# Folding the conditioning sums from 128 lanes to 64 before they are transposed

## The reference

```
def adaln(cond, w_ada, b_ada):
    return jnp.split(jax.nn.silu(cond) @ w_ada + b_ada, ADA_CHUNKS, axis=-1)

m_lat = [m[:, None, :] for m in adaln(c, w_ada[l], b_ada[l])]
m_ctx = adaln(c_ctx, w_ada[l], b_ada[l])
```

## Time and profile before

| | us |
|---|---|
| median of 3 runs | 2838.33 (2838.24 to 2838.36) |
| the profiled execution | 2838.6 |
| its span from first to last instruction | 2837.0 |
| PE busy in it | 2818.5 |
| DVE busy | 2005.0 |
| ACT busy | 1365.0 |

### The profile page before, as it was taken

One profiled execution on the slowest core, in us unless ns is written; L12 is line 12 of the kernel. 1 busy time (PEld: TensorE's weight loads), 2 busy tenths in 40 slices (PEclk: granted clock), 3 DMA queues, 4 the chain that ended last, 5 costly groups with the idle time before them and its releaser, 6 DMA issues.

```text
span 2837.0 us, 33955 instructions
## 1 busy us (share of the span) xinstructions
PE 2818.5 (99%) x13151; PEld 2333.5 (82%) x13151; DVE 2005.0 (71%) x2614; ACT 1365.0 (48%) x1733; POOL 23.5 (1%) x47
## 2 busy tenths in 40 slices
PE   9999999999999999999999999999999999999999
PEld 7888888888888888788888788888878888888887
DVE  6876799999877668756647888877765655655444
ACT  6655544444443447632334666654454444444333
POOL 2000000000000000000000000000000000000000
PEclk9999999999999999999999999999999999999999
DMA  7545687887878778456646544457767777776564
GB/s 258 151 134 178 186 258 251 255 257 248 259 248 271 268 256 264 147 160 189 178 145 187 151 120 126 119 188 260 232 191 228 223 223 226 225 228 201 191 192 153
DMA packets 299952, 583.18 MB, mean 206 GB/s; under 512 B 18394, under 2 KB 18802, under 8 KB 299153
## 3 DMA queue, kind: packets, MB, share of 16 engines
q1 hardware_dynamic: 296896, 572.01, 64.6%
q0 software_dynamic: 2320, 7.96, 0.9%
q10 hardware_dynamic: 576, 1.05, 0.1%
HBM read 578.85 MB, written 2.10 MB: 205 GB/s over the span
## 4 chain that ended last, share of the span: by engine, by line
PE 94%; DVE 3%; ACT 1%; issue 1%; DMA 1%; SPq 0%; ACTq 0%; DVEq 0%
PE psum L566 22%; PE psum L563 22%; PE psum L565 22%; PE psum L636 3%; PE psum L638 3%; PE psum L637 3%; PE psum L3099 2%; PE psum L3101 2%; PE psum L3100 2%; PE psum L511 1%; PE psum L513 1%; PE psum L512 1%; PE psum L3119 1%; PE psum L591 1%; PE psum L3159 1%
## 5 line engine op out<-in xcount | busy, mean ns | idle before, releaser
L719 DVE TENSOR_TENSOR w_lo<-w_raw,w_hi 128x1024 fp32r<-128x1024 f32 x776 | 945.7, 1223 | 607.8 <-ACT w_hi L713 603.9
L713 ACT ACTIVATE w_hi<-w_raw 128x1024 fp32r<-128x1024 f32 x776 | 821.9, 1060 | 1085.1 <-PE psum L566 1015.7
L563 PE MATMUL psum<-w_hi,x_split 128*128 128x512 f32 x1880 | 737.3, 392 | 0.0
L566 PE MATMUL psum<-w_hi,x_split 128*128 128x512 f32 x1880 | 732.3, 390 | 0.0
L565 PE MATMUL psum<-w_lo,x_split 128*128 128x512 f32 x1880 | 731.8, 389 | 0.0
L566 PEld LDWEIGHTS psum<-w_hi,x_split 128*128 128x128 f32 x1880 | 352.9, 188 | 73.7
L563 PEld LDWEIGHTS psum<-w_hi,x_split 128*128 128x128 f32 x1880 | 353.1, 188 | 71.6 <-DVE x_split L2597 0.3
L565 PEld LDWEIGHTS psum<-w_lo,x_split 128*128 128x128 f32 x1880 | 353.2, 188 | 71.5
L563 PE MATMUL psum<-w_hi,hidden_split 128*128 128x512 f32 x704 | 274.9, 390 | 0.0
L566 PE MATMUL psum<-w_hi,hidden_split 128*128 128x512 f32 x704 | 274.0, 389 | 0.0
L565 PE MATMUL psum<-w_lo,hidden_split 128*128 128x512 f32 x704 | 273.9, 389 | 0.0
(11 more groups left out here) (405 smaller groups left out, 3619.1 us busy)
## 6 DMA issues: line engine op xcount, KB each, us to landing
w_raw<-in_w_in SPq DMA_DIRECT2D x216, 512.0 KB, 3.6
w_raw<-in_w_ada SPq DMA_DIRECT2D x192, 512.0 KB, 4.8
w_raw<-in_w_ffn_up SPq DMA_DIRECT2D x176, 512.0 KB, 4.5
w_raw<-in_w_ffn_down SPq DMA_DIRECT2D x88, 512.0 KB, 5.5
w_raw<-in_w_ff_gate SPq DMA_DIRECT2D x88, 512.0 KB, 4.2
w_raw<-in_w_ff_up SPq DMA_DIRECT2D x88, 512.0 KB, 4.2
w_raw<-in_w_ff_down SPq DMA_DIRECT2D x88, 512.0 KB, 4.7
w_raw<-in_w_out SPq DMA_DIRECT2D x64, 512.0 KB, 4.7
```

The costliest lines, as they stand in the source:

```text
L563: nc.tensor.matmul(to, x_hi[:, tokens], hi, start=u == 0 and t == 0, stop=False, skip_group_check=True)
L566: mm = nc.tensor.matmul(to, x_lo[:, tokens], hi, start=False, stop=end and t == 1, skip_group_check=True)
L713: nc.scalar.activation(w_hi[:, b.slot(n)], raw[:, b.raw_slot(k)], ACT.Copy).then_inc(w_rounded, 1)
L719: nc.vector.tensor_tensor(w_lo[:, slot], raw[:, b.raw_slot(k)], r(w_hi[:, slot]), ALU.subtract).then_inc(w_split, 1)
```

## The change

Before a sum is transposed, its 128 partitions are folded to 64. The 512 columns are seen as two halves of 256. ScalarE copies the upper 64 partitions of the first half to the lower 64 of a new tile, and the lower 64 partitions of the second half to its upper 64 (step at+1, after its rounding). VectorE adds to these the other 64 partitions of each half (step at+2, after its remainder). The tile is 128x256 and holds two column blocks in each transpose: TensorE transposes two blocks instead of four, still in step at+3, and now waits for the folded tile instead of the last part of the sum. VectorE's last reductions (step at+4) read 256 columns instead of 512. The next group's first part waits for the folding on VectorE itself instead of the transposes. The second condition's tile lies in columns of `TAB` that are unused at that time.

```diff
@@ ada_turn (TensorE, step at+3)
-                    pe.wait_ge(w_split, b.load(b.last_part[i]) + RAW + 1)
+                    pe.wait_ge(S("ada_folded"), b.ada_group(i) + 1)
                     pe.wait_ge(ada_evacuated, b.ada_group(i) + 1)
                     for v in range(b.conditions(i)):
-                        for f in range(NF):
-                            ins = nc.tensor.transpose(PS[:, 6 + v, f * P:f * P + P],
-                                                      ada_sum(b, i, v)[:, f * P:f * P + P], const("ident"))
+                        for h in range(2):
+                            ins = nc.tensor.transpose(PS[:, 6 + v, h * P:h * P + P],
+                                                      ADA_FOLD[v][:, h * P:h * P + P], const("ident"))
                     ins.then_inc(ada_turned, 1)
@@ stream_act, stream_act_tokens (ScalarE, each step, after the rounding)
+                ada_shift(act, b, n)
@@ ada_unit (VectorE)
                     if b.ada_freed(i) > 0:
-                        dve.wait_ge(ada_turned, b.ada_freed(i))
+                        dve.wait_ge(S("ada_folded"), b.ada_freed(i))
@@ new
+        def ada_shift(act, b, n):
+            for i, at in enumerate(b.done):
+                if n == at + 1:
+                    act.wait_ge(w_split, b.load(b.last_part[i]) + RAW + 1)
+                    if b.ada_group(i) > 0:
+                        act.wait_ge(ada_turned, b.ada_group(i))
+                    for v in range(b.conditions(i)):
+                        total = ada_sum(b, i, v)
+                        nc.scalar.activation(ADA_FOLD[v][0:64], total[64:P, 0:256], ACT.Copy)
+                        ins = nc.scalar.activation(ADA_FOLD[v][64:P], total[0:64, 256:512], ACT.Copy)
+                    ins.then_inc(S("ada_shifted"), 1)
+
+        def ada_fold(dve, b, n):
+            for i, at in enumerate(b.done):
+                if n == at + 2:
+                    dve.wait_ge(S("ada_shifted"), b.ada_group(i) + 1)
+                    for v in range(b.conditions(i)):
+                        total, to = ada_sum(b, i, v), ADA_FOLD[v]
+                        nc.vector.tensor_tensor(to[0:64], to[0:64], total[0:64, 0:256], ALU.add)
+                        ins = nc.vector.tensor_tensor(to[64:P], to[64:P], total[64:P, 256:512], ALU.add)
+                    ins.then_inc(S("ada_folded"), 1)
+                    folded.append(i)
@@ ada_evac (VectorE, step at+4)
-                        ins = nc.vector.tensor_reduce(MADA[:, b.ada_cols[i] * NF:(b.ada_cols[i] + 1) * NF, v],
-                                                      PS[:, 6 + v, :].rearrange("p (f n) -> p f n", f=NF),
+                        to = MADA[:, b.ada_cols[i] * NF:(b.ada_cols[i] + 1) * NF, v]
+                        ins = nc.vector.tensor_reduce(to.rearrange("p (s h) -> p h s", h=2),
+                                                      PS[:, 6 + v, 0:2 * P].rearrange("p (h s l) -> p h s l", h=2, s=2),
                                                       AX.X, ALU.add)
@@ stream_dve, stream_dve_tokens (VectorE, each step, after the remainder)
+                ada_fold(dve, b, n)
```

More of the change, by code:

```diff
@@ L312, in build @@
         ST = sb("stat", [P, 512])
+        FOLD = sb("fold", [P, 256])
         PS = ctx.enter_context(nc.psum_tensor("psum", [P, 8, 512], F32))
@@ L394, in build @@
         ADA_SUM = ST[:, 0:GC], SM[:, 96:96 + GC]
+        ADA_FOLD = FOLD, TAB[:, 0:256]
         def ada_sum(b, i, v):
@@ L738, in ada_unit @@
                 if u == 0 and t == 0:
+                    assert len(folded) >= b.ada_freed(i)
                     if b.ada_freed(i) > 0:
-                        dve.wait_ge(ada_turned, b.ada_freed(i))
+                        dve.wait_ge(S("ada_folded"), b.ada_freed(i))
                 elif t == 0:
@@ L751, in ada_unit @@
                 ins.then_inc(ada_half if t == 0 else w_split, 1)
+        folded = []
+        def ada_shift(act, b, n):
[19 more added lines that the diff above has]
+                    folded.append(i)
         def ada_evac(dve, b, n):
```

## The result

Five runs of the changed kernel took 2888.88 us in the median (2888.32 to 2892.55), the kernel before 2838.33 (2837.24 to 2840.33): a ratio of 1.0179, 95% interval 1.0167 to 1.019. Slower was right; the size was not. I had 28 us more and a range that ended at 2877; it is 50 us more.

A forecast was written before the change was run, and what follows sets the result against it. PE, busy 99% of the span, was taken to bound the kernel. Delays of 5.9 + 2.5 + 1.9 + 24.7 = 35.0 us, less 7.0 us of transposes, gave net +28.0: 2866.3 us, range 2858 to 2877.

The forecast's parts named there:

- What bounds, and the step that decides: PE, busy 99% of the span; VectorE's remainder ends 0.14 us before the transposes, so the additions make PE wait.
- The transposes: On PE, 128 transposes become 64 at 0.109 us each: 7.0 us less, all on the path.
- The restart and the form of the delay: At PE's turn: additions' end plus 0.06, less the earlier transpose start, plus 0.07 us; nothing where negative.
- Quiet groups: Nine one-condition groups (down 1 to 3, branch 0 and 1, up2 0 to 3): 0.65 us delay each, 5.9 us.
- The additions and copies: VectorE additions 0.76 us for one condition, 1.44 for two; ScalarE copies 0.62 and 1.24, hidden in quiet one-condition groups.
- Up 4 and down 0: Two-condition groups, delayed by 4.3 us (copies push the convolution's first taps) and 3.4 us (two square sums follow).
- rival (a): PE's clock falls in the new waits; +14 us, 2880, if all eight two-condition groups pay; chance 0.08 for all eight.
- Nothing else late: Behind each delay PE has three units ready; later token-tile turns have over 2 us of cover, so no further loss.

The follow-up runs named there:

- the sets of four: The kernel before, with added 256-column copies and additions, four in a row, in quiet steps of phase down2, results unread: 2837.14 us.
- one experiment: The changed kernel with only the sixteen one-condition groups folded, the eight two-condition groups the old way: 2849.71 us, ratio 1.0035, +10.3 where +7.5 was forecast.

## Why the prediction was right and wrong

- **What bounds, and the step that decides.** Right. That "loop at+2" on VectorE begins when PE is already at at+3, that the remainder ends 0.14 us before the transposes, and that the additions therefore make PE wait in 19 places and not in kv: all as read. Moving the transposes by one and by two units confirms it.
- **The transposes**, 64 x 0.109 = 7.0 us: right, shown by the kernel with the transposes two steps later, where only the gain is left, and by kv in the changed kernel, where eight fewer take 0.87 us off PE. The estimate from the Trainium skill (TensorE: Matmul & The Clock Gate, section Back-to-back issue gap), 5.2 us, would have been low.
- **The restart and the form of the delay**: right. Quiet groups 0.74 for 0.65, and the 0.09 is the one gap between two additions, 0.43 for 0.34.
- **The additions and copies**: mis-sized, by a condition that my rows didn't have. My neighbours were instructions of full height; the fold's alternate between halves. Four copies are 1.72 for 1.24, the three gaps of four additions 1.29 for 1.02: 0.75 us for each two-condition group behind the copies. That is up 0 (3.75 for 3.0), up 5 (3.71), up 6 (3.01) to the tenth. The bounds (copies 0.27 to 0.45) held the copies but not the additions (0.27 to 0.40).
- **Up 4 and down 0**: right in their place as the longest, short by 1.9 and 1.2 us. At up 4, VectorE's convolution starts at 644.85, 1.05 us after ScalarE's first tap and behind its second; I had it start behind the first. That is 0.5; copies and additions give 0.75; and 0.6 is low clock, which the delay's measure touches: from the first transpose to the second matmul behind takes 1.34 us there, 0.72 at up 0. At down 0 copies and additions give 0.75 and low clock 0.2; the last 0.2 wasn't traced.
- **The clock, rival (a)**: the step that failed. My sum had nothing for it, and I gave it 0.08 and argued that "most waits are shorter than that at the start", as if the wait had to be as long as the one of 4.7 us that I had a row for. That row can't bear this. It is the start of the program, where no full clock is on record before; and between the wait of 4.7 us and the slow matmuls PE did 5.4 us of smaller ones. It gave the price of a slow stretch and nothing on how long a wait brings one on; runs showed falls from 2.6 us of idle time on, and eight of eight in the changed kernel. The price was right: 1.7 us forecast, 1.6 measured, 14 for eight, 13.1 measured. Taken as the likeliest, it would have made the forecast 2880, and with the 7.8 us by which the waits were too short 2888. A fall at the end of phase gates, 1.6 us, was in no term.
- The rule behind it in the Trainium skill (TensorE: Matmul & The Clock Gate, Part 1: The HAM clock gate), that idle time lowers the clock, is what the trace then showed.
- **Nothing else late**: right; no other wait of PE on another engine changed.

## What to carry to other kernels

Before a wait is put in front of the bounding engine, write down at what moment of that engine's own work the loops of the others begin: a loop index that is one less isn't a unit earlier, and here moving the consumer by two units turned +50 us into -6. Then price a stall of TensorE as its length plus the lower clock behind it, and look at the clock and at the spacing of the starts in an experiment, not at its time alone. An overlap between neighbours that is read from full-height instructions doesn't hold for ones that alternate between halves of the lanes.

## What the runs showed of the hardware

- After the start, the granted clock fell at every idle time of TensorE of 3.08 us and more (3.2 to 5.8 us in the changed kernel; 3.08 at up 4 with the transposes one step later) and at none of 2.4 us or less. In between it went either way: it fell behind 2.64 us (up 6 without the second copies) and 2.86 (gate 0 in the run with six idle matmuls), not behind 2.77 to 2.84 (gate 0 in four other kernels) or 3.05 (up 5 without the second copies). So the length isn't all that counts there; what else does wasn't tried. In the changed kernel the low clock began 0.5 to 1.4 us after PE was back and lasted 3.4 us; at up 4 it began 2.2 us before PE was back and lasted 6.8.
- Idle time isn't even needed. In eight of the ten profiled executions (not in that of the kernel before, nor in that with the sets of four) the clock falls at the end of phase gates, behind or within 32 matmuls of one column that take 3.6 to 4.6 us; in six it also falls at some 235 us, as 16 such matmuls end or up to 1.1 us later. Both of those without a fall at the gates have the old transposes throughout, so whether the change has a part in it is open. The timeline of the changed kernel:

```profile
1911.94 3.86 PE L3210 MATMUL psum<-constants,region_b 128*128 128x1 f32 x32
1915.67 0.77 PE L566 MATMUL psum<-w_hi,x_split 128*128 128x512 f32 x1
1916.24 0.63 PE L568 MATMUL psum<-w_lo,x_split 128*128 128x512 f32 x1
```

In the profiled execution of the kernel before the same place ran at full clock (starts 0.23 apart from 1872.41 us on). But fifteen executions of that kernel went from 2836.06 us, at a mean granted clock of 1.000, to 2843.13, at 0.998, so the clock falls in some of them too; where isn't on record. That spread, and the 2.8 us by which one experiment was over its count, are about what a change of 0.2% is worth here, and a single profile of such a kernel should be asked for its clock before it is compared.

And an idle matmul of plain float32, 128x512, occupies TensorE for 0.86 us in two rows at full granted clock, where a matmul of the split weights takes 0.23.
